# Second kind of mixer in another order: index columns first, softmax units between projection units, sticks alone last

## What is computed

```python
proj = h @ w_in[layer]
(qa, ka, va, qb, kb, vb, qi, ki, wi, qc, kc, vc) = jnp.split(proj, split_points, axis=-1)
...
oa = moba_attention(qa, ka, heads(va, N_HEADS_A))
ob = dsa_attention(qb, kb, heads(vb, N_HEADS_B), qi, ki, wi)
oc = stick_breaking_attention(heads(qc, N_HEADS_C), heads(kc, N_HEADS_C), heads(vc, N_HEADS_C))

o = jnp.concatenate([oa, ob, oc], axis=2)
o = (_rms(o).reshape(B, S, D_MIX) * out_g[layer].astype(jnp.float32)).astype(x.dtype)
x = x + g2 * (o @ w_out[layer])
```

## Time and profile before

| what | before |
|---|---|
| median of 3 runs | 2540.73 us (2540.01 to 2544.52) |
| the profiled execution | 2543.67 us, span 2542.0 us |
| granted TensorE clock, mean | 0.998 |
| TensorE busy | 2507.8 us, 99% |
| VectorE busy | 2077.4 us, 82% |
| ScalarE busy | 1580.2 us, 62% |
| GpSimd busy | 203.0 us, 8% |

### The profile page before, as it was taken

One profiled execution on the slowest core, in us unless ns is written; L12 is line 12 of the kernel. 1 busy time (PEld: TensorE's weight loads), 2 busy tenths in 40 slices (PEclk: granted clock), 3 DMA queues, 4 the chain that ended last, 5 costly groups with the idle time before them and its releaser, 6 DMA issues.

```text
span 2542.0 us, 44424 instructions
## 1 busy us (share of the span) xinstructions
PE 2507.8 (99%) x17392; PEld 2271.8 (89%) x17392; DVE 2077.4 (82%) x2845; ACT 1580.2 (62%) x2315; POOL 203.0 (8%) x275
## 2 busy tenths in 40 slices
PE   9999999999999999999999999999999999999999
PEld 9999998999999999999997999987999899987998
DVE  5688767999999999999998898575898888575665
ACT  5644556888888888888886544455544544455543
POOL 2111021000000000000000011021011011021000
PEclk9999999999999999999999999999999999999999
DMA  7698536999999999999997786432786686431542
GB/s 297 235 361 307 202 139 257 384 368 376 370 371 372 369 374 369 379 370 374 370 394 290 257 320 243 167 107 92 260 323 262 257 315 240 166 109 51 207 183 75
DMA packets 136639, 696.56 MB, mean 274 GB/s; under 512 B 16528, under 2 KB 16656, under 8 KB 87728
## 3 DMA queue, kind: packets, MB, share of 16 engines
q1 hardware_dynamic: 109872, 599.12, 63.1%
q0 software_dynamic: 23424, 88.16, 9.1%
q10 hardware_dynamic: 3136, 6.43, 0.7%
HBM read 683.61 MB, written 13.24 MB: 274 GB/s over the span
## 4 chain that ended last, share of the span: by engine, by line
PE 91%; DVE 4%; ACT 2%; issue 1%; POOL 1%; DMA 0%; DVEq 0%; ACTq 0%; POOLq 0%
PE ps L2342 16%; PE ps L1916 16%; PE ps L1917 15%; PE ps L1918 15%; PE ps L2504 11%; PE ps L2344 8%; DVE w_parts L1640 1%; PE ps L1944 1%; PE ps L2474 1%; PE ps L1940 1%; ACT w_parts L1080 1%; DVE a_parts L1648 1%; PE ps L2152 1%; PE ps L2258 1%; DMA ring<-wstream 0%
## 5 line engine op out<-in xcount | busy, mean ns | idle before, releaser
L2342 PE MATMUL ps<-a_parts,w_parts 128*128 128x512 f32 x1760 | 618.7, 393 | 0.3
L1640 DVE TENSOR_TENSOR w_parts<-ring,w_parts 128x1024 fp32r<-128x1024 f32 x448 | 548.4, 1224 | 53.9 <-ACT w_parts L1080 52.9
L1916 PE MATMUL ps<-w_parts 128*112 128x256 f32 x1792 | 515.4, 288 | 0.0
L1918 PE MATMUL ps<-w_parts 128*112 128x256 f32 x1792 | 498.5, 278 | 0.0
L1917 PE MATMUL ps<-w_parts 128*112 128x256 f32 x1792 | 498.4, 278 | 0.0
L2344 PE MATMUL ps<-a_parts,w_parts 128*128 128x256 f32 x1760 | 492.6, 280 | 0.0
L1080 ACT ACTIVATE w_parts<-ring 128x1024 fp32r<-128x1024 f32 x448 | 471.9, 1054 | 0.7 <-DMA ring<-wstream 0.6
L2342 PEld LDWEIGHTS ps<-a_parts,w_parts 128*128 128x128 f32 x1760 | 329.8, 187 | 73.8 <-issue 2.9
L2344 PEld LDWEIGHTS ps<-a_parts,w_parts 128*128 128x128 f32 x1760 | 332.3, 189 | 0.0
L1916 PEld LDWEIGHTS ps<-w_parts 128*112 128x112 f32 x1792 | 312.9, 175 | 11.8 <-issue 0.2
L1917 PEld LDWEIGHTS ps<-w_parts 128*112 128x112 f32 x1792 | 312.7, 174 | 11.8
(11 more groups left out here) (273 smaller groups left out, 4635.1 us busy)
## 6 DMA issues: line engine op xcount, KB each, us to landing
ring<-wstream SPq DMA_DIRECT2D x378, 1024.0 KB, 7.2
ring<-wstream SPq DMA_DIRECT2D x378, 512.0 KB, 5.8
proj<-astream POOLq DMA_DIRECT2D x144, 512.0 KB, 5.6
slot_rows<-branch POOLq DMA_DIRECT2D x7, 448.0 KB, 7.2
slot_out<-slot_rows POOLq DMA_DIRECT2D x1, 3136.0 KB, 14.8
sq<-slot_rows ACTq DMA_DIRECT2D x49, 64.0 KB, 5.5
slot_out<-pT ACTq DMA_DIRECT2D x49, 64.0 KB, 5.3
cst<-consts SPq DMA_DIRECT2D x1, 1692.0 KB, 14.2
```

The lines of the kernel that those rows point to most:

```text
L1640: nc.vector.tensor_tensor(up_lo[:, n % 2, at], ring[:, s, at], up_hi[:, n % 2, at], ALU.subtract)\
L1916: mm(o, stationary[0], moving[0], start=start, stop=False, skip_group_check=True)
L1918: return mm(o, stationary[1], moving[0], start=False, stop=stop, skip_group_check=True)
L2342: mm(ps[:, bank, :], hi, a_parts[:, :, k, :], start=k == 0, stop=k == KB - 1, skip_group_check=True)
```

## The change

- The columns of `w_in` are laid out in another order (`F_ORDER`, `IN_TILES`): blocks 8 to 12 (index queries and keys) first, then the four softmax groups, then stick queries and keys in turn; the first value tile, which holds the index weights, comes third. Rotation, index scores and top-eight rounds move with them.
- The softmax units stand between projection units on each engine: scores of unit 0 behind projection unit 20, the last turning and values behind the projection.
- The sticks alone stand last, behind the projection, other PSUM banks and buffers in hand. Their helpers are named `logits`, `tails` (the running sums) and `weigh`. Between them stand the head sums, root, spread and scale of the softmax blocks 0 to 3 and the split of the second output tile.
- The output projection starts with blocks 0 to 3; the blocks of the sticks follow. Every `fill` of these mixers is gone. Squares are taken on ACT from PSUM beside each copy.

PE in the sticks, before: one head and the start of the next. L2277 and L2279 are logits, L2152 is `fill`, L2311 to L2313 the running sums, L2291 and L2292 the weighing of the head two before.

```diff
-            [("f", i) for i in range(5)] + [("v", 0), ("f", 5), ("f", 6), ("v", 1), ("v", 2)])
+            [("f", 0), ("f", 1), ("v", 0), ("f", 2), ("f", 3), ("f", 4), ("v", 1), ("f", 5), ("f", 6), ("v", 2)])
...
+F_ORDER = (8, 9, 10, 11, 12, 0, 1, 2, 3, 4, 5, 6, 7, 13, 17, 14, 18, 15, 19, 16, 20)
+INDEX_JOBS = {8: (0, 1), 9: (2, 3), 10: (4, 5), 11: (6, 7), 12: (8, 9, 10, 11), 13: (12, 13, 14, 15)}
+ROPE_JOBS = {4: (0,), 5: (1,), 6: (2,), 17: (3,), 18: (4,), 19: (5,), 20: (6,)}
+SPREAD_JOBS = {16: (0, 1), 17: (2, 3)}
...
+                exps(u)
+                in_copies(m, 21, 23)
+                exps(u + 1)
+                copy_turned(u)
+                in_copies(m, 23, 24)
+                copy_out(u, 0)
+                in_copies(m, 24, 25)
+                exps(u + 2)
+                copy_turned(u + 1)
+                in_copies(m, 25, 26)
+                copy_out(u + 1, 0)
+                log_term(m, 0)
+                in_copies(m, 26, 27)
+                copy_turned(u + 2)
+                exps(u + 3)
+                log_term(m, 1)
+                copy_out(u + 2, 2)
+                log_term(m, 2)
+                stick_exp(m, 0)
+                copy_turned(u + 3)
+                log_term(m, 3)
+                stick_exp(m, 1)
+                copy_out(u + 3, 2)
+                hi_half(out, 1, 0)
+                log_term(m, 4)
+                stick_exp(m, 2)
+                copy_sticks(m, 0)
+                first_root(m)
+                log_term(m, 5)
+                stick_exp(m, 3)
+                hi_half(out, 1, 1)
+                log_term(m, 6)
+                stick_exp(m, 4)
+                copy_sticks(m, 1)
+                cat_hi(m, range(2))
+                log_term(m, 7)
+                stick_exp(m, 5)
+                cat_hi(m, range(2, 4))
+                stick_exp(m, 6)
+                copy_sticks(m, 2)
+                stick_exp(m, 7)
+                copy_sticks(m, 3)
...
+                divided(u)
+                masked(u + 1, C("cmask1"))
+                lo_tiles(stage, [9])
+                take_eight(14)
+                take_eight(15)
+                allowed(1)
+                divided(u + 1)
+                masked(u + 2, select[0][:, :])
+                for h in range(2):
+                    lo_outproj(m, 0, h)
+                divided(u + 2)
+                masked(u + 3, select[1])
+                softplus(0)
+                softplus(1)
+                divided(u + 3)
+                exponent(0)
+                softplus(2)
+                exponent(1)
+                softplus(3)
+                exponent(2)
+                lo_outproj(m, 1, 0)
+                softplus(4)
+                exponent(3)
+                softplus(5)
+                exponent(4)
+                cat_scaled(m, 0)
+                cat_scaled(m, 1)
+                lo_outproj(m, 1, 1)
+                softplus(6)
+                exponent(5)
+                cat_scaled(m, 2)
+                cat_scaled(m, 3)
+                softplus(7)
+                exponent(6)
+                for k in range(2):
+                    cat_rest(m, k)
+                exponent(7)
+                for k in range(2, 4):
+                    cat_rest(m, k)
...
+                if n == 20:
+                    pe.wait_ge(qk_ready, 8 * (l + 1))
+                    pe.wait_ge(rope_ready, len(PAIRS) * l + 5)
+                    scores(u, 0, 0, 2)
+                if n == 21:
+                    scores(u + 1, 1, 0, 2)
+                if n == 22:
+                    pe.wait_ge(rope_ready, len(PAIRS) * (l + 1))
+                    turned(u, 0)
+                if n == 23:
+                    pe.wait_ge(in_copied, before + 19)
+                    values(u, 0, IDX)
+                    scores(u + 2, 0, 4, 6)
+                if n == 24:
+                    turned(u + 1, 1)
+                if n == 25:
+                    scores(u + 3, 1, 4, 6)
+                    logits(m, 0)
+                    values(u + 1, 1, IDX)
+                if n == 26:
+                    turned(u + 2, 0)
+                    logits(m, 1)
...
+                    pe.wait_ge(sp_ready, 8 * (m - 1))
+                    blocks(0, 0)
+                    blocks(0, 1)
+                    cat_sums(m, 1)
+                    blocks(0, 2)
+                    blocks(0, 3)
+                    blocks(1, 0)
+                    cat_spread(m, 2)
+                    cat_spread(m, 3)
+                    for p in range(1, CAT_FIRST):
+                        blocks(1, p)
                 for i in range(2):
-                    for p in range(CAT_FIRST[0], KB):
+                    for p in range(CAT_FIRST, KB):
                         blocks(i, p)
...
+            def cat_spread(m, j):
+
+                l = m - 2
+                pe.wait_ge(root_ready, 3 * l + j // 2 + 2)
+                if j in (1, 3):
+                    pe.wait_ge(cat_ready, KB * m + 2 * j)
+                for k in (2 * j, 2 * j + 1):
+                    ins = mm(ps[:, cat_bank(k), (k % 2) * T:(k % 2 + 1) * T],
+                             C("spread")[0:16, k * P:(k + 1) * P], sq[0:16, 2 + j // 2, :], start=True, stop=True)
+                ins.then_inc(spread_ready, 1)
...
+                values(u + 2, 0, IDX + 256)
+                logits(m, 2)
+                tails(m, 0)
+                turned(u + 3, 1)
+                logits(m, 3)
+                tails(m, 1)
+                weigh(m, 0)
+                values(u + 3, 1, IDX + 256)
+                logits(m, 4)
+                tails(m, 2)
+                weigh(m, 1)
+                logits(m, 5)
+                tails(m, 3)
+                cat_sums(m, 0)
+                weigh(m, 2)
+                logits(m, 6)
+                tails(m, 4)
+                weigh(m, 3)
+                cat_spread(m, 0)
+                logits(m, 7)
+                tails(m, 5)
+                weigh(m, 4)
+                cat_spread(m, 1)
+                tails(m, 6)
+                weigh(m, 5)
+                tails(m, 7)
+                weigh(m, 6)
+                weigh(m, 7)
+                outproj1(m)
```

More of the change, by code:

```diff
@@ L1373, in cat_norm @@
             def cat_norm(m):
[L1375 to L1381 removed]
+                first = CAT_FIRST
+                if m < 2:
                     dve.wait_ge(cat_root, 2 * m + 2)
@@ new lines, in mixer2 @@
+                for i in range(4):
+                    indexed(i)
+                lo_tiles(stage, [5])
+                for i in range(4, 8):
+                    indexed(i)
+                for i in range(2):
+                    take_eight(i)
+                for i in range(8, 12):
+                    indexed(i)
+                lo_tiles(stage, [6])
+                for i in range(12, 16):
+                    indexed(i)
+                for i in range(2, 8):
+                    take_eight(i)
@@ new lines, in mixer2 @@
+                allowed(0)
+                qk_scaled(range(4))
+                lo_tiles(stage, [7])
+                take_eight(8)
+                qk_scaled(range(4, 8))
+                roped(3)
+                take_eight(9)
+                lo_tiles(stage, [8])
+                roped(4)
+                take_eight(10)
+                roped(5)
+                take_eight(11)
+                masked(u, C("cmask0"))
+                roped(6)
+                take_eight(12)
+                take_eight(13)
@@ L2253, in mixer1, with head_sums @@
                 outproj1(m)
-            def head_sums(ready, squares, blocks, first=True, last=True, at=0):
-                for i, b in enumerate(blocks):
-                    ins = mm(SS[0:16, at:at + T], C("headsel")[:, b * 16:(b + 1) * 16], squares[:, b, :],
-                             start=first and i == 0, stop=last and i == len(blocks) - 1,
-                             skip_group_check=True)
-                if last:
-                    ins.then_inc(ready, 1)
+            def head_sums(ready, o, squares):
+                for i, (b, sq_b) in enumerate(squares):
+                    ins = mm(o[0:16, 0:T], C("headsel")[:, b * 16:(b + 1) * 16], sq_b,
+                             start=i == 0, stop=i == len(squares) - 1)
+                ins.then_inc(ready, 1)
@@ new lines, in tails @@
+            def tails(m, h):
+                nn = 8 * (m - 2) + h
+                if h == 0:
+                    pe.wait_ge(s_used, 4 * m + 4)
+                elif h == 1:
+                    pe.wait_ge(pt_copied, 4 * m + 4)
+                else:
+                    pe.wait_ge(arg_ready, nn - 1)
+                pe.wait_ge(spm_ready, nn + 1)
+                a = ps[:, after_bank(h), :]
+                spm = st_d[:, nn % 2, 2, :]
+                mm(a[:, 0:T], C("after"), spm[:, 0:T], start=True, stop=False)
+                mm(a[:, P:T], ones[:, :], spm[:, T:T + P], start=False, stop=True)
+                mm(a[:, T:T + P], C("after"), spm[:, T:T + P], start=True, stop=True).then_inc(af_ready, 1)
```

527 lines of the change are left out of this document (194 added, 333 removed).

## The result

The changed kernel takes 2570.11 us (median of 4 runs, 2569.05 to 2572.91) against 2540.69 for the kernel before: ratio 1.0114, 95% interval 1.0097 to 1.0132, so 29.4 us more. The profiled execution has a span of 2568.0 us. Slower was forecast, with 2554; 2570 lies above the range of 2536 to 2568.

A forecast was written before the change was run, and what follows sets the result against it. TensorE, busy 99% of the span, was taken as the bound. Per mixer 8.8 + 44.3 + 27.7 = 80.8 against 80.2 and 78.7 us gives +2.7; clock +10.5 makes +13.2: 2554 us, range 2536 to 2568.

The forecast's parts named there:

- projection: Input projection: 7.4 us of added TensorE softmax and logits work plus waits of 0.85 and 0.55, +8.8 us a mixer.
- sticks in place of sticks and softmax, full clock: Stretch behind the projection: 44.3 us in place of 28.2 (sticks) and 23.2 (softmax units).
- output projection, full clock: Output projection: products 23.0, head sums 1.8, two spreads 1.8, wait 1.0, making 27.7 us against 28.8 and 27.2.
- clock: Sticks into output projection: TensorE's clock halves in gaps without fills, 6.1 and 4.4 us in the two mixers, +10.5.
- Items 1 to 5: Sticks: the in-order waits and closing chain that spread VectorE's eight softplus pairs and end the stretch at 44.3 us.
- Item 1: Sticks start: last unit's division stands behind softplus 1; TensorE idles 3.7 us before turning; softplus 4 at 17.7.
- Items 2, 3 and 5: Sticks: root ahead of log term 5 (softplus 5 at 22.7); scales ahead of softplus 6 (30.2); closing chain to 44.3.
- item 4: Late sticks: the same ring of scales waiting for the spread, without the tile, ahead of softplus 7, at 36.1 us.
- items 1 and 2: Sticks: waits from softplus 1 ahead of the division and the root ahead of log term 5; softplus 5 at 22.7.
- items 3 and 4: Sticks: scales waiting for the spread stand ahead of softplus 6 and 7, which come at 30.2 and 36.1 us.
- the longest gap: Sticks: TensorE idle for 4.1 us ahead of the values of head 4, bringing the one clock drop counted.
- The rival with the clock low through most of the sticks: Sticks: TensorE steps on the path double, 16 us a mixer; +36.4 in all, 2577 us, chance 0.1.

The follow-up runs named there:

- a_fills: Changed kernel plus 34 filler products a mixer in TensorE's gaps, ahead of the last unit's turning and the values of heads 2, 3, 4, 5, 7: 2559.0 us.
- a_proj: Changed kernel with its three projection waits taken out (divisions of units 0 and 1 earlier, copy of turned unit 0 ahead of unit 1's exponentials): 2568.9 us.
- b_nofill: Kernel before without the fills of its two second-kind mixers, 23 a mixer, nothing else changed: 2554.4 us.
- a_order_proj: Changed kernel, no fills, with last unit's division, first root and scales of blocks 0 to 3 moved and the three projection waits taken out: 2542.4 us.
- a_all: a_order_proj plus the second step of block group 1 set between the two spreads in the output projection, no fills: 2539.2 us.
- f_div_root: Changed kernel with last unit's division ahead of softplus 1, first root behind log term 5 and exponential 3, plus 27 fills a mixer: 2554.4 us.

## Why the prediction came out as it did

The direction was right, and so were both mechanisms, the in-order waits and the fall of the clock in gaps that had no fill. The sum was 16 us short, and each of its four terms was too small, the clock by most. In us over both mixers:

| term | predicted | measured | from |
|---|---|---|---|
| projection | +17.6 | +21.7 | marks to 1701.4: 109.4 became 120.2 |
| sticks in place of sticks and softmax, full clock | -14.3 | -10.9 | a_fills, second mixer: 46.0 |
| output projection, full clock | -0.6 | +2.4 | the same: 29.2 |
| clock | +10.5 | +16.5 | the rest of 29.7 |

- **Projection, +8.8 a mixer; it was +10.9.** The prediction laid two waits of together 1.4 us; the profile has three, 0.63 + 1.44 + 0.68 = 2.75. The one that it did not have is the 0.63 ahead of the turning of unit 0, whose division stands behind two top-eight rounds; the copy behind four exponentials was sized at 0.85 and took 1.44. The other 0.7 us is the added work itself, a tenth dearer than laid. a_proj moved what TensorE waited for and won 1.7 us a mixer.
- **Sticks, 44.3; they were 46.0 at full clock.** Items 1 to 5 stand in the trace in their order, and moving what they name moved the time. The mis-sized pieces are small. Item 1 priced the division like one that runs alone, 1.23 us; it took 2.04 (below). Items 2, 3 and 5 were each 0.3 or 0.4 longer, item 4 0.1. Undone at full clock, items 1 and 2 gave about 4.5 us and items 3 and 4 at least 4.2, against the 4 to 5 laid for each pair. Without fills, part of that was lost to the clock.
- **Output projection, 27.7; it was 29.2.** "Before, two head sums, two spreads and two fills stood there, about as much work, so nothing comes from this side" is the sentence that failed: the second mixer's went from 27.2 to 29.2. TensorE's timeline of before, from 2316.9 on, has only these beside the 192 products:

```profile
2318.13 1.04 PE L2258 MATMUL ps<-branch,cst 128*16 128x256 f32 x4
...
2324.68 1.13 PE L2246 MATMUL ps<-sq,cst 16*128 16x256 f32 x4
2325.74 1.13 PE L2152 MATMUL ps<-cst,ones 128*128 128x256 f32 x4
```

  Sums over two blocks, one pair of spreads and two fills, 3.3 us; the other sums and spreads came earlier. After, sums over four blocks (1.90), two pairs of spreads (1.13 + 1.10) and the wait of 1.06 stand there, 5.2 us. The sum of 27.7 itself was short in every piece: the products took 23.5 and not 23.0, the two spreads 2.2 and not 1.8, and the way from the last product to the residual 0.6 and not 0.1. Weaving products into the wait gave 0.9 back (28.3).
- **Clock, +10.5; it was +16.5.** This is the step that failed by most. "I take the drop that the longest gap brings and that lasts into the output projection" chose one of several gaps. The trace has three falls a mixer: already the first gap of 4.00 us brought one of 10 us, the second lasted 20 and the third 3.4, together 34 us that cost 8.3 us a mixer (203.7 against 195.4), where 6.1 were laid. The rival with the clock low through most of the sticks (2577) had the place right and a chance of 0.1 only; its 16 us a mixer were twice what the low clock cost, since much of the low time lay under TensorE's waits. There is a slip in the arithmetic too: the 1.7 us that the first mixer already paid before are inside the 80.2 us that the full-clock sum was held against, and were taken off a second time. Without the slip the forecast would have been 2556.

Of the signs that the prediction named, three held: the two widest distances between softplus pairs are those ahead of the seventh and the eighth, TensorE idled 4.00 us ahead of the last unit's turning, and the granted clock was 0.50 in the second half of the sticks. The others came out too small: the projection ends 10.8 us later and not 7 to 10, the softplus pairs are spread over 43.5 us (38.3 at full clock) and not 33 to 40, and the stretch from the last L2348 takes 31.0 and not 27. The gap ahead of the values of head 4 was only 2.47 us, because the sums ahead of it ran at half clock.

The Trainium skill, TensorE: Matmul & The Clock Gate, section "Why this matters for your kernels", warns of a long idle gap between bursts of matmuls. The first fall, behind 4.00 us, agrees with it. The second, at 1731, came behind two shorter ones, 0.87 and 2.56 us with small products between them. That one is nearer to the swing by short idles that the prediction cites from the Trainium skill.

## What to carry to other kernels

When a reordering deletes filler matmuls, first lay out the gaps and ask for every gap, not for the longest, what the clock does behind it; here the fills of two mixers were worth 11.7 us in the old order and 11 to 13 in the new. Judge in-order waits at full clock: with the clock free to fall, two edits gave 2.8 and 3.1 to 6.3 us a mixer alone and 12 together, at full clock about 4.2, 4.5 and 7.8. Check in the trace that each fill ends before what it waits for; four that did not hid 1.8 us of a gain. And before a stretch is called unchanged, list its instructions in the trace of before; the output projection, called unchanged, grew by 2.0 us.

## What the runs showed of the hardware

- **A microsecond at half clock has no fixed price.** Low time of 34.1 us cost 8.3 us (after against a_fills, second mixer), 0.24 each; 23.9 us cost 6.9 in the old order (b_nofill against before, second mixer), 0.29, if the fills that went cost nothing. In the output projection, which is nearly all products, 3.4 us cost 1.5 and 6.8 us cost 3.0 (30.7 and 32.2 against 29.2), 0.44 each. Where TensorE waits for others anyway, its half rate lies under the wait. A fill can leave its wait at half clock: in the first mixer of a_fills the nine fills of head 4 took 5.1 us in place of 4.1 and put off the values by 1.4.
- **Equal code did not fall equally.** With the first gap filled the second fall lasted 27 us in one mixer and 20 in the other. And with the wait of 1.06 us in the output projection a fall began there in 17 of 20 profiled mixers, without it in none of 4. That this wait is the cause is likely, not shown: between the closest pair of runs, a_order_proj and a_all, it is 1 of 2 against 0 of 2.
- **A VectorE operation can slow down beside GpSimd.** The division L1382, 128x1024 elements from two operands in the shared memory, took 1.23 us in f_div_root, where GpSimd had nothing to do yet, and 2.03 in the changed kernel. It took 2.03 or 2.04 in all twelve mixers in which a GpSimd product had just begun, and 1.22 or 1.23 everywhere else. GpSimd's timeline there:

```profile
1707.33 1.00 POOL L627 TENSOR_TENSOR branch<-branch,cst 128x384 f32<-128x384 f32 x1 [4.41 <-DVE branch L1517]
```

  Its mask product runs beside the first half of the division (1707.37). The Trainium skill, GPSIMD Engine Reference, section "Specifications", says that GpSimd contends with VectorE instructions that have two such inputs; the rows agree, with 0.8 us for a product of 1.0. Which of the two begins first seems to decide who pays: in the first block the same division begins 0.24 us ahead of a GpSimd sum of 128x1024 (L600) and keeps its 1.23 us, while the sum takes 2.75, where one of 128x768 that begins ahead of VectorE's work takes 1.47.
